# The partition swap of a rotary embedding: four copies on ScalarE, or four transfers within SBUF

## What is computed

```python
def apply_rope(x, cos, sin):
    x1, x2 = jnp.split(x, 2, axis=-1)          # 32 + 32 of the 64 features of a head
    c, s = cos[None, :, None, :], sin[None, :, None, :]
    return jnp.concatenate([x1 * c - x2 * s, x2 * c + x1 * s], axis=-1)

q = apply_rope(rms_norm(q, q_norm_g[l]), cos, sin) * q_scale
k = apply_rope(rms_norm(k, k_norm_g[l]), cos, sin)
```

## Time and profile before

| | |
|---|---|
| median of 3 runs | 1054.87 us (1054.68 to 1055.4) |
| profiled execution | 1054.45 us, span 1052.6 us |
| TensorE busy | 1038.3 us, 99% of the span |
| VectorE, ScalarE, GpSimd busy | 685.3, 464.7, 104.0 us |
| mean granted clock of TensorE | 0.997 |
| shifts on ScalarE | 40 copies of 32 x 528, 640 to 646 ns each |

### The profile page before, as it was taken

One profiled execution on the slowest core, in us unless ns is written; L12 is line 12 of the kernel. 1 busy time (PEld: TensorE's weight loads), 2 busy tenths in 40 slices (PEclk: granted clock), 3 DMA queues, 4 the chain that ended last, 5 costly groups with the idle time before them and its releaser, 6 DMA issues.

```text
span 1052.6 us, 18739 instructions
## 1 busy us (share of the span) xinstructions
PE 1038.3 (99%) x7896; PEld 991.6 (94%) x7896; DVE 685.3 (65%) x1019; ACT 464.7 (44%) x707; POOL 104.0 (10%) x108
## 2 busy tenths in 40 slices
PE   8999999999999999999999999999999999999998
PEld 7998999999999999999999989999889998899987
DVE  6768545669855599455547784655797557975452
ACT  6986435334323443223338773443442334423322
POOL 1252001110001100011003510000000000000000
PEclk9999999999999999999999999999999999999999
DMA  7220322231333222322321203232223332233212
GB/s 236 92 66 17 121 81 80 81 105 57 121 101 101 81 81 81 120 82 90 94 97 51 81 8 114 81 112 88 81 81 120 102 100 80 80 121 90 92 60 80
DMA packets 94107, 94.96 MB, mean 90 GB/s; under 512 B 3424, under 2 KB 92856, under 8 KB 94024
## 3 DMA queue, kind: packets, MB, share of 16 engines
q1 hardware_dynamic: 93456, 93.58, 27.8%
q10 hardware_dynamic: 312, 0.18, 0.1%
q0 software_dynamic: 256, 0.01, 0.0%
HBM read 91.65 MB, written 2.10 MB: 89 GB/s over the span
## 4 chain that ended last, share of the span: by engine, by line
PE 84%; DVE 9%; ACT 4%; issue 2%; DVEq 0%; ACTq 0%
PE slot L568 65%; PE slot L974 12%; PE slot L785 2%; PE slot L626 1%; ACT sumsq L1245 1%; PE slot L1034 1%; PE slot L845 1%; PE slot L852 1%; DVE ms_work L1635 1%; PE slot L817 1%; DVE w_lo L421 1%; DVE k_dup L1647 1%; DVE nmax L1698 1%; DVE m_op_lo L1904 0%; DVE sink_arg L1703 0%
## 5 line engine op out<-in xcount | busy, mean ns | idle before, releaser
L568 PE MATMUL slot<-x_hi,w_hi 128*128 128x264 f32 (+2 forms) x1516 | 354.6, 300 | 0.0
L568 PE MATMUL slot<-x_lo,w_hi 128*128 128x264 f32 (+2 forms) x1516 | 350.5, 298 | 0.0
L568 PE MATMUL slot<-x_hi,w_lo 128*128 128x264 f32 (+2 forms) x1516 | 350.1, 298 | 0.0
L568 PEld LDWEIGHTS slot<-x_hi,w_hi 128*128 128x128 f32 x1516 | 246.3, 189 | 11.3 <-issue 0.7
L568 PEld LDWEIGHTS slot<-x_lo,w_hi 128*128 128x128 f32 x1516 | 245.0, 189 | 7.3
L568 PEld LDWEIGHTS slot<-x_hi,w_lo 128*128 128x128 f32 x1516 | 244.8, 189 | 7.5
L421 DVE TENSOR_TENSOR w_lo<-raw,w_hi 128x2048 fp32r<-128x2048 f32 (+2 forms) x68 | 151.3, 2225 | 99.2 <-ACT w_hi L410 99.2
L410 ACT ACTIVATE w_hi<-raw 128x2048 fp32r<-128x2048 f32 (+2 forms) x68 | 124.0, 1823 | 150.7 <-PE slot L568 95.5
L1138 POOL TENSOR_TENSOR work<-work 128x528 f32<-128x528 f32 (+1 forms) x32 | 42.0, 1312 | 707.3 <-DVE work L1864 348.5
L1421 ACT ACTIVATE work<-gate,par_all 128x528 f32<-128x528 f32 (+1 forms) x44 | 31.9, 731 | 135.2 <-DVE gate L1591 68.2
L974 PE MATMUL slot<-m_op_hi,w_hi 128*128 128x264 f32 (+1 forms) x256 | 73.8, 288 | 1.3 <-DVE h L1940 0.7
(11 more groups left out here) (217 smaller groups left out, 1670.2 us busy)
## 6 DMA issues: line engine op xcount, KB each, us to landing
raw<-in_w_gate SPq DMA_DIRECT2D x44, 512.0 KB, 4.7
raw<-in_w_up SPq DMA_DIRECT2D x44, 512.0 KB, 4.7
raw<-in_w_down SPq DMA_DIRECT2D x32, 512.0 KB, 4.0
raw<-in_w_in SPq DMA_DIRECT2D x19, 512.0 KB, 4.9
raw<-in_w_out SPq DMA_DIRECT2D x16, 512.0 KB, 4.0
raw<-in_w_down SPq DMA_DIRECT2D x16, 384.0 KB, 3.6
x_in<-in_x SPq DMA_DIRECT2D x4, 512.0 KB, 6.5
out<-y_out SPq DMA_DIRECT2D x4, 256.0 KB, 2.4
```

The costliest lines, as they stand in the source:

```text
L568: ins = nc.tensor.matmul(out_part, w[ws][:, r, cols], a[:, k, tokens], start=first and n == 0 and w is w_hi and a is a_hi, stop=end and w ...
```

## The change

`shift(n)` starts four transfers from ScalarE's queue in place of its four copies. A transfer counts 16 on its semaphore when it has landed, so `rots_ready` counts 64 for a shift where it counted 1, and all who wait for it are changed to match. ScalarE no longer does the swap itself in its own order, and so `q_tile`, which overwrites what `q_squares` reads, gets a wait for the squares of its own (before, the wait for the shift behind them covered it).

```diff
--- before.py
+++ after.py
@@ -1099,7 +1099,7 @@
                     pool.wait_ge(evac[ps.slot(name)], ps.before(name, l) + 1)
                     pool.wait_ge(qtab_ready, l + 1)
                     steps.link(nc.gpsimd.tensor_tensor(rot_c[:], head[:, j % 2], q_cos, ALU.mult))
-                    pool.wait_ge(rots_ready, l * 5 + (n + 1))
+                    pool.wait_ge(rots_ready, 64 * (l * 5 + (n + 1)))
                     kv, cols = j // 2, slice(j % 2 * CHUNK, (j % 2 + 1) * CHUNK)
                     chunks = [r[:, N_META:].rearrange("p (b q) -> p b q", q=CHUNK) for r in (rot_c, rot_s[n % 2])]
                     nc.gpsimd.tensor_tensor(q_rot[:, kv, 0, cols], rot_c[:, 0:CHUNK], rot_s[n % 2][:, 0:CHUNK], ALU.add)
@@ -1242,8 +1242,7 @@
                     if n > 1:
                         act.wait_ge(*rotated_before(l, n - 1))
                     for to, fr in ((0, 32), (32, 0), (64, 96), (96, 64)):
-                        ins = nc.scalar.activation(rot_s[n % 2][to:to + 32], sine[fr:fr + 32], ACT.Copy)
-                    ins.then_inc(rots_ready, 1)
+                        act.dma_start(rot_s[n % 2][to:to + 32], sine[fr:fr + 32]).then_inc(rots_ready, 16)
 
                 def pooled_hi(n):
                     act.wait_ge(pooled_ready, l * 4 + (n + 1))
@@ -1593,6 +1592,7 @@
                 def q_tile(j):
                     if j >= 2:
                         dve.wait_ge(q_ready, l * 4 + (j - 1))
+                        dve.wait_ge(headsq_ready, l * 5 + j)
                     scaled(f"q{j}", head[:, j % 2])
 
                 rot = Chain(dve, dve_rot, l, 2)
@@ -1601,7 +1601,7 @@
 
                     name = ROTATED[n]
                     if n > 0:
-                        dve.wait_ge(rots_ready, l * 5 + n)
+                        dve.wait_ge(rots_ready, 64 * (l * 5 + n))
                     if name == "k":
                         dve.wait_ge(headn_ready, l + 1)
                         nc.vector.tensor_tensor(sine, k_dup[:, 0], sin, ALU.mult).then_inc(sine_ready, 1)
@@ -1640,7 +1640,7 @@
                 split_lo(dve, l, 3)
                 sine_part(2)
                 dve.wait_ge(rotc_ready, l + 1)
-                dve.wait_ge(rots_ready, l * 5 + 2)
+                dve.wait_ge(rots_ready, 64 * (l * 5 + 2))
                 for kv in range(N_KV_HEADS):
                     src = slice(kv * HEAD_DIM, (kv + 1) * HEAD_DIM)
                     for half in range(2):
```

## The result

| | before | after |
|---|---|---|
| median of the runs | 1055.13 us (4 runs, 1054.68 to 1055.81) | 1060.43 us (4 runs, 1059.15 to 1061.17) |
| ratio, 95% interval | | 1.005 (1.0038 to 1.0062) |
| profiled execution | 1054.45 us | 1061.16 us |
| its span | 1052.6 us | 1059.4 us |

The kernel became 5.3 us slower. The forecast was 1053.7 us and its range ended at 1058.4, so the time lies above it: a loss where a small gain was forecast.

A forecast was written before the change was run, and what follows sets the result against it. The chain was taken as 84% TensorE, gaining only where it waits: 0.80 us earlier less 0.20 overlap gives 0.60 us a layer, 1.2 in all, from 1054.87 to 1053.7 us; 8-in-10 range 1052.3 to 1058.4.

The forecast's parts named there:

- the price of a start: How long starting one transfer takes ScalarE's queue: taken as 0.377 us, with 0.28 and 0.63 kept as bounds.
- the landing: Time one 66 KB transfer within SBUF needs to land: taken as 2.0 us, bounds 1.9 and 2.6.
- The split's lateness: ScalarE's weight split of unit 4 after shift 4: forecast 0.80 us earlier than before in the first layer.
- T: Time from a shift's begin until its last quarter lands: 3.13 us (2.7 to 4.5) in place of 2.61.
- I: Time ScalarE is taken by a shift's four starts: 1.51 us (1.1 to 2.5) in place of 2.61.
- e: Delay of shift 4's begin: what T exceeds 3.22 us by, plus what it exceeds 3.74 us by.
- i: Time one transfer's start takes ScalarE's queue: 0.377 us taken; four make up I, three enter T.
- the first rival: Late landings at shifts 1, 3 and 4 make the kernel slower, cases from 1058.8 to 1062.4 us; chance 0.27.
- excess over 3.74: At shift 0, k's sine product was held to be on time up to T = 3.74 us; anything beyond adds delay.
- The overlap: VectorE's split of unit 4 beside GpSimd's last sum for 0.6 us: cost taken as 0.2 us (0 to 0.5).
- The step from ScalarE to TensorE: VectorE's row to `pool_lo` 0.60 us earlier per layer, fitting TensorE's listed waits of 0.2 + 0.6 and 0.6 us.
- The clock: TensorE's low-clock stretches behind `q_means(1)` and `scores(0)` might shrink: up to 2.9 us more gained, 1050.8; chance 0.10.

The follow-up runs named there:

- one start a shift: Kernel after with one 128-partition transfer per shift in place of four, the swap of halves left out: 1052.34 us, ratio 0.9979 to the kernel before.
- all on SyncE's queue: Kernel after with all four transfers of each shift started by SyncE instead of ScalarE: 1058.98 us, ratio 1.0039 to the kernel before.
- half copies: Kernel after with each shift done as two copies on ScalarE and two transfers started by SyncE: 1053.28 us, ratio 0.9985 to the kernel before.

## Why the prediction was wrong

**The step that failed** is the price of a start: "I take 0.377, the middle one of a series started in a row". It is 0.61 us (0.51 for the first). The upper end, 0.626 from the same row, was the right one; the landing, 2.0, was right. The weighing went by nearness, as if a start's price hung on its place in a row of small loads from memory; nothing in the rows said so. The split's lateness, T + I + e - 5.44, holds i seven times, and thirteen times once both excesses in e count, so 0.23 us in one start turns 0.8 us early into 1.5 us late: with i = 0.61 the formula gives T = 3.83, I = 2.44, e = 0.70. It came out as the first rival, at 1060.4 where that rival's nearest case had 1058.8.

**What the runs make of the formula.** Measured were 65.15 - 62.07 = 3.1 us in the first layer, less 0.6 of start-up 2.5. From one shift's begin to the next the profiles before and after have, in the first layer, 3.94 and 5.71 us from shift 1 to 2, 4.73 and 4.72 from 2 to 3, 3.60 and 4.65 from 3 to 4. So the loss enters at shifts 1 and 3, as the formula has it, and nothing at 2; 1.1 of the 1.8 us at shift 1 are its slow start, which the formula doesn't hold. Its excess over 3.74, for shift 0, did not come: that shift's starts went out at 39.79, ahead of the square root (40.27) and of the squares that stand before them in ScalarE's order, where the copies had begun at 41.08. In the second layer, without a slow start, shift 4 began 1.2 us late and the split 1.0. That the formula with 0.61 comes near both layers is in part luck, since these terms go against each other.

**The overlap** of VectorE's split with GpSimd's last sum was taken too low: 0.2 us for 0.6 us side by side, since the split of 2.79 us was read as "full overlap". GpSimd's product beside it ended at 47.62, 0.64 us after that split began:

```profile
45.95 1.67 POOL L1096 TENSOR_TENSOR rot_c<-k_dup,cst 128x528 f32<-128x528 f32 x1
```

So these 0.5 us are the price of 0.6, and the gain forecast for a layer would have been 0.3 and not 0.6.

**The step from ScalarE to TensorE** had two faults. Its limit was the length of the listed waits; one start a shift gained more than these (the map 1.5 us earlier, the wait for `pool_lo` still 0.6), because the time at which TensorE comes to the wait moves too. And a late split was felt first at `q_means(1)`, by way of the squares of q3 behind shift 4 on ScalarE, not at `pool_lo` and not at `scores(0)`. I had listed the 0.2 us wait for `head_sq` as something to gain; a wait that is already there is also the place where any delay enters in full.

**The clock** was a rival only on the gaining side. In the first layer it came out on the other: the low stretch grew from some 3.5 us to 10. With the slow start it is what lies beyond the formula; how much of the loss it would have to itself is not separated.

**Right:** the new wait costs nothing; shifts 0 and 2 are covered (the first by going out early, which was not foreseen); shifts 1, 3 and 4 are the ones in series, and the loss is there; `scores(0)` waits next, once `q_means(1)` doesn't.

**What the Trainium skill says.** The Trainium skill, "DMA: Bandwidth & Descriptors", section "Anatomy of one DMA", gives by its figures, as an estimate, 2.16 us for 66 KB, though its fit is for transfers from GpSimd. The landings agree roughly: 2.0 us in the median.

The Trainium skill's section "Rules for kernel authors" on the same page advises to join many small transfers into one, and calls those under 64 KB mostly overhead; these have 66. The advice was the better guide here, though by another price, the starts: one transfer of 264 KB landed in 2.4 to 2.7 us, where four of 66 KB had all landed only after 3.9.

## What to carry to other kernels

Price a row of transfers by starts first: here one within SBUF cost nearly as much as a copy of 32 x 528 on ScalarE (0.61 against 0.64 us), so a transfer in place of a short copy freed next to nothing and brought its result most of a landing later. Where a small price enters the sum seven or thirteen times, let the forecast follow the less favourable row, or split the chance evenly between the sides. Don't take the length of a listed wait for the most that an earlier release can give: the waiting engine may come earlier too. And where a swap stands in series with itself, try halving its length on each of two engines (two copies beside two transfers were 1.8 us faster than before) rather than moving it whole.

## What the runs showed of the hardware

A start of a transfer within SBUF of 32 partitions took 0.51 us as the first of a row and 0.59 to 0.61 as a later one, on SyncE's and on ScalarE's queue; one of 128 partitions and four times the bytes took 0.47. While SyncE started two transfers too, two on ScalarE's queue took 1.42 us in place of 1.15. Starts on ScalarE's queue went out ahead of activations that stand before them in its order (39.79 against 40.27 us), while activations behind a row of starts came after it (64.47 behind 64.42).

VectorE's split of 128 x 2048 and GpSimd's operations did not share the time in which they overlapped; the one that began later took longer by nearly the whole of it. Splits begun under a GpSimd operation ended 2.14 to 2.15 us behind that operation: before (47.62 to 49.77), after (67.56 to 69.70), one start a shift (62.67 to 64.82), all on SyncE's queue (62.52 to 64.67), half copies (63.34 to 65.49); alone such a split took 2.29. The sum that had begun first kept its 1.28 us. GpSimd's product, begun under the split in the SyncE run, ended 1.16 us behind it, against 1.30 alone.

TensorE's low clock came in one layer of a profile and not in another of the same kernel (0.93 and 1.00 over 580 to 604 us in the two profiles of the kernel after), at the same total time; a single profile's low stretch is therefore a weak term for a forecast.
